# The per-chunk norm of a bidirectional scan: variance spread by its own product, root and reciprocal at full width

## The chip, the cores and the metric

The kernel runs on one core of a Trainium2 chip. The metric is the device time of one execution, in microseconds. TensorE (PE in the profile, its weight loads PEld), VectorE (DVE), ScalarE (ACT), GpSimd (POOL) and the DMA queues work in parallel and are kept in order by semaphores alone; on each engine instructions run in the order in which the program lists them.

## What is computed

One layer of a hybrid backbone over 1024 latent and 128 context tokens, 1024 channels, 16 heads of 64, all in fp32. The part that matters here is the norm at the end of the token mixer's scans:

```
wkv = ys[0] + ys[1]                     # forward and backward scan
mu = jnp.mean(wkv, axis=-1, keepdims=True)          # over a head's 64 channels
var = jnp.mean(jnp.square(wkv - mu), axis=-1, keepdims=True)
ln = ((wkv - mu) * lax.rsqrt(var + LNX_EPS)).reshape(B, T, D_RWKV) * p['lnx_w'] + p['lnx_b']
x_a = (ln + (bonuses[0] + bonuses[1]).reshape(B, T, D_RWKV)).astype(xn.dtype) * g_out
```

Around it stand the input projections ahead of the scans and, behind them, the output projections and the MLP.

## The kernel before

**Stages.** Projections of eight pairs of heads (to about 1035 us of the span), the scans (1035 to 1640 us), then dense products. Only the scans are touched, and of them only the norm.

**The scans.** A pair of heads is 128 channels, which lie on the 128 partitions, head 0 on the upper 64 and head 1 on the lower. Time is cut into NC = 9 chunks of C = 128 tokens, eight latent and one context. A unit is a pair and a chunk position; there are UNITS = 72, and both directions of a unit are done together. One software-pipelined loop, `for s in range(-4, UNITS)`, is written out for every engine: step s does the serial part of unit s, the Gram products of unit s + 4, and inverse work of the units between. With j = s mod 9, TensorE's order in a step is: turn (transposes into inv), token_major (transposes into bank 3), ur_state (the state's product, ser<-state,ub), gram of direction 0 (gbank<-ub), serial_ur (ser<-vb,gmat), **spread**, left (inv<-xtb), y_state (ser<-ub,state), gram of direction 1, serial_u, right, **mean**, serial_s, serial_y, **gate**, **variance**.

**The norm of a chunk.** `finals(s)` names the chunk whose y is complete in step s, one a step from s = 5 on (67 units); the last five are done in a tail behind the loop (`TAIL`). Per chunk, y is yf, 128 channels by 128 tokens:
- TensorE, mean: ones within a head (bones) times y, so that the sum stands on all 64 channels of the head (place(n, 0) in bank 2). VectorE, centred (L2180): y minus the mean. ScalarE, squares_of (L1675): the square into fsq, a ring of five buffers.
- TensorE, variance: fsq as the stationary operand and two columns of bones as the moving one. The result has the tokens on the partitions and the two heads as columns: 128x2, in two columns at the end of bank 2 (`column(n)`).
- ScalarE, deviation (L1681), at the start of the next step: the square root, 128x2, into fstd. VectorE, reciprocal (L2184): 128x2, in place.
- TensorE, spread, in the next step: each column of fstd, repeated 64 times, times the identity, which gives 1/deviation for every channel and token (place(n, 1) in bank 2). VectorE, scaled: y times that (L2189), weight and bonus (L2193), bias and gate (L2196), then the chunk goes out by DMA.

**What sets the order around it.** VectorE's order in step s: reciprocal of the last step's chunk, y_add (L2168, the sum of the two directions' y, for units with j = 4 to 7; the others are copied by ScalarE, L1666), turned (L2114), carried (L2142), the Gram mask of direction 0 (L2108), the three operations of scaled, summed (L2125), centred, states (L2157), the Gram mask of direction 1. In steps 9 to 23 a forward substitution for the last pair (L2029, L2036) is laced in, around scaled. TensorE's ur_state and first Gram product wait until the y of the unit before is out (yd_ok or ya_ok), its second Gram product for the mask of direction 0 (gram_ok), its y_state for ScalarE's copy of ur (ur_ok, L1651), its serial_u for GpSimd's triangle products (tri_ok, L898).

In the tail the five chunks go stage by stage: five means, five centrings, five squares, five gates, five variances, five roots, five reciprocals, five spreads, and then, behind all five spreads, five times scaled. The dense products need the last one's result.

The matmuls go through a helper and all bear L970; the tiles tell them apart.

## Time and profile before

| | before |
|---|---|
| median of 3 runs | 2705.92 us (2702.68 to 2709.07) |
| the profiled execution: time / span | 2705.67 us / 2703.6 us |
| busy in the span | PE 2580.1, PEld 2430.1, DVE 1852.0, ACT 1080.2, POOL 1175.8 us |
| granted TensorE clock, mean | 0.985 |
| the scans | 1035 to 1640 us of the span |

All durations come from the profiled execution, whose own time lies 0.25 us below the median. Matmuls are pipelined and up to four small ones run on different parts of the array at once, so a row's mean duration is not what it costs; the starts of the weight loads (PEld) show the pace. An fp32 product is two records, a product over both heads four.

### The profile page before, as it was taken

The page shows a single profiled execution, that of the slowest core. Times are in us where ns is not written, and L with a number is a line of the kernel's source. Part 1 is how long each engine was busy: PE and PEld are TensorE (multiplying, and loading weights), DVE is VectorE, ACT ScalarE, POOL GpSimd, SP SyncE. Part 2 cuts the span into 40 slices and gives each one's busy share as a digit, 9 for nine tenths or more (in the row PEclk, how much of TensorE's full clock was granted, in tenths as well). Part 3 has the DMA queues.
Part 4 walks back from the last instruction along what each step waited for, and adds up shares of the span by engine and source line. Part 5 has one row for each costly group of instructions (what it writes and reads, how often), then busy time and mean ns, then how long its engine had stood idle before and what let it go on. Part 6 is the DMA issues. An engine that isn't in the chain of part 4 may idle for free.

```text
span 2703.6 us, 68164 instructions
## 1 busy us (share of the span) xinstructions
PE 2580.1 (95%) x28864; PEld 2430.1 (90%) x28864; DVE 1852.0 (68%) x3010; ACT 1080.2 (40%) x1978; POOL 1175.8 (43%) x1154
## 2 busy tenths in 40 slices
PE   4899999999999998999999997999799999999998
PEld 3899999999999996788878887999799999999998
DVE  3464665846748464787766666799778679678686
ACT  3434243342433422433333343443453353443534
POOL 1323222322223224555555544656446556565662
PEclk8999999999999999999999999999899999999999
DMA  8333425435254363444454456454223232333231
GB/s 323 106 110 109 144 69 181 125 97 158 62 174 128 94 193 108 131 143 144 138 154 137 139 160 195 131 175 105 63 63 79 81 101 70 79 84 102 65 79 71
DMA packets 282412, 329.15 MB, mean 122 GB/s; under 512 B 76288, under 2 KB 215936, under 8 KB 273536
## 3 DMA queue, kind: packets, MB, share of 16 engines
q1 hardware_dynamic: 274448, 278.66, 33.2%
q0 software_dynamic: 5904, 39.32, 6.9%
q10 hardware_dynamic: 1760, 6.82, 0.6%
q8 instruction: 231, 3.78, 0.6%
q14 instruction: 69, 0.57, 0.1%
HBM read 221.83 MB, written 91.36 MB: 116 GB/s over the span
## 4 chain that ended last, share of the span: by engine, by line
PE 85%; DVE 7%; issue 2%; DMA 2%; ACT 2%; SPq 1%; POOL 0%; DVEq 0%; ACTq 0%; POOLq 0%
PE ser L970 18%; PE gbank L970 13%; PE bank L970 11%; PE inv L970 11%; PE gbank L1411 8%; PE inv L1411 8%; PE ser L1411 7%; PE bank L1411 7%; DVE a_sum L2298 1%; DMA ring<-in_wblocks 1%; PE inv L1172 1%; PE bank L1155 1%; DVE a_sum L2302 1%; DVE a_sum L2306 1%; DVE a_lo L2272 1%
## 5 line engine op out<-in xcount | busy, mean ns | idle before, releaser
L952 POOL TENSOR_TENSOR w_lo<-raw_w,w_hi 128x512 fp32r<-128x512 f32 x264 | 425.3, 1624 | 370.2 <-ACT w_hi L1747 370.1
L847 POOL TENSOR_TENSOR wsp<-ring,wsp 128x1024 fp32r<-128x1024 f32 x67 | 210.8, 3146 | 670.7 <-ACT wsp L1513 670.7
L1747 ACT ACTIVATE w_hi<-raw_w 128x512 fp32r<-128x512 f32 x264 | 165.1, 632 | 262.5 <-PE ser L1411 98.4
L970 PE MATMUL ser<-xn_hi,wsp 128*128 128x384 f32 x816 | 217.7, 340 | 6.1 <-POOL xn_lo L853 6.1
L1411 PE MATMUL gbank<-a_hi,w_hi 128*128 128x288 f32 x616 | 185.7, 302 | 30.6 <-POOL w_lo L952 14.6
L970 PE MATMUL gbank<-xn_hi,wsp 128*128 128x384 f32 x800 | 213.0, 339 | 1.1 <-issue 1.1
L970 PE MATMUL bank<-xn_hi,wsp 128*128 128x384 f32 x800 | 211.1, 338 | 2.2 <-POOL wsp L847 2.2
L970 PE MATMUL inv<-xn_hi,wsp 128*128 128x384 f32 x800 | 211.3, 338 | 0.5 <-issue 0.5
L2108 DVE TENSOR_TENSOR gmat<-gbank,gmask 128x1024 f32<-128x1024 f32 x144 | 175.6, 1219 | 49.8 <-PE gbank L970 49.0
L1733 ACT ACTIVATE a_hi<-a_sum 128x1152 fp32r<-128x1152 f32 x88 | 103.1, 1173 | 224.6 <-DVE a_sum L2306 78.0
L970 PE MATMUL gbank<-ub 64*64 64x128 f32 (+1 forms) x3456 | 178.4, 310 | 9.5 <-DVE gmat L2108 5.6
L1411 PE MATMUL gbank<-a_hi,w_lo 128*128 128x288 f32 x616 | 184.7, 300 | 0.0
L1411 PE MATMUL gbank<-a_lo,w_hi 128*128 128x288 f32 x616 | 184.4, 299 | 0.0
L1411 PE MATMUL inv<-a_hi,w_lo 128*128 128x288 f32 x616 | 183.9, 299 | 0.0
L1411 PE MATMUL inv<-a_hi,w_hi 128*128 128x288 f32 x616 | 183.7, 298 | 0.0
L1411 PE MATMUL inv<-a_lo,w_hi 128*128 128x288 f32 x616 | 183.6, 298 | 0.0
L1411 PE MATMUL ser<-a_hi,w_hi 128*128 128x288 f32 x616 | 181.6, 295 | 1.5 <-ACT r L1786 1.5
L1411 PE MATMUL bank<-a_hi,w_lo 128*128 128x288 f32 x616 | 181.8, 295 | 0.0
L1411 PE MATMUL ser<-a_hi,w_lo 128*128 128x288 f32 x616 | 181.7, 295 | 0.0
L1411 PE MATMUL ser<-a_lo,w_hi 128*128 128x288 f32 x616 | 181.4, 294 | 0.0
L1411 PE MATMUL bank<-a_lo,w_hi 128*128 128x288 f32 x616 | 181.4, 294 | 0.0
L1411 PE MATMUL bank<-a_hi,w_hi 128*128 128x288 f32 x616 | 181.3, 294 | 0.0
(398 smaller groups left out, 7534.7 us busy)
## 6 DMA issues: line engine op xcount, KB each, us to landing
ring<-in_wblocks SPq DMA_DIRECT2D x107, 512.0 KB, 4.8
ub<-op_d SPq DMA_DIRECT2D x144, 256.0 KB, 2.8
raw_w<-in_wquads SPq DMA_DIRECT2D x33, 1024.0 KB, 4.8
raw_w<-in_wquads POOLq DMA_DIRECT2D x22, 1024.0 KB, 8.8
op_d<-ar SPq DMA_DIRECT2D x32, 576.0 KB, 5.4
op_d<-bk SPq DMA_DIRECT2D x32, 576.0 KB, 6.2
raw_w<-in_wquads SPq DMA_DIRECT2D x44, 256.0 KB, 3.3
raw_w<-zsum POOLq DMA_DIRECT2D x11, 1024.0 KB, 12.3
```

What stands on the lines that cost most here:

```text
L847: GT(wsp[s % 2][1][:], ring[(N_ADA_RING + s) % RING][:], wsp[s % 2][0][:].bitcast(F32), ALU.subtract).then_inc(S["wsplit_lo"], 1)
L952: GT(w_lo[n % 4][:], src, w_hi[n % 4][:].bitcast(F32), ALU.subtract).then_inc(S["wl_ok"], 1)
L970: return nc.tensor.matmul(out, lhsT, rhs, start=start, stop=stop)
L1155: ins = nc.tensor.transpose(banks[3][:, y * P:(y + 1) * P], ub[v % LOADS][:, y // 2, 2 + y % 2, :], ident[:])
L1172: ins = nc.tensor.transpose(inv[:, 0, x * P:(x + 1) * P], xt[:, place_of(v), :, :].rearrange("p h t -> p (h t)"), ident[:])
L1411: return nc.tensor.matmul(out, lhsT, rhs, start=start, stop=stop, skip_group_check=True)
L1733: A(a_hi[:, places2(q, j), :], src, ACT.Copy).then_inc(S["ah_ok"], 1)
L1747: A(w_hi[s][:], raw_of(op)[:, m, :].rearrange("p (k c) -> p k c", k=KH), ACT.Copy).then_inc(S["wh_ok"], 1)
L2108: V.tensor_tensor(gmat[v % SETS][:, d, :, :, :].rearrange("p h x t -> p h (x t)"), gbank[:, :, :], gmask[:, d:d + 1, :].to_broadcast([P, 2 ...
L2272: V.tensor_tensor(a_lo[:, places2(q, j), :], src, a_hi[:, places2(q, j), :].bitcast(F32), sub).then_inc(S["al_ok"], 1)
L2298: ch.step(V.tensor_tensor(o[j], a11[j], a12[j], sub))
L2302: ch.step(V.tensor_tensor(o[j], o[j], a22[j], add))
```

## The change

- **variance** takes bones (the 64x64 block of ones of a head) as the stationary operand and fsq as the moving one: as in the mean, the sum stands on all 64 channels of the head, 128x128, in place(n, 1) of bank 2 (in the tail in banks 4 and 5).
- **deviation** reads that, takes the root of 128x128 and writes it over fsq, whose squares have been used. squares_of waits for the buffer's last user now, where deviation did.
- **reciprocal** works on 128x128 in fsq, in place.
- **spread** is gone, with its wait for the reciprocal, its ring fstd and its place in the tail; scaled multiplies by fsq from SBUF and waits for the reciprocal, which runs on its own engine.

The diff, without the declaration of fstd, the calls of spread and a semaphore count in a later norm that follows from it:

```
-            def column(n):
-
-                i = n - TAIL[0][2]
-                return banks[2][:, 4 * P - 2:4 * P] if i < 0 else ser[:, 1, 2 * i:2 * i + 2]
-
             def variance(p, c, n):
                 pe.wait_ge(S["ysq_ok"], n + 1)
-                for b in halves_of:
-                    ins = mm(column(n)[b, :], fsq[:, n % 5, b], bones[:, 0:P:HD], True, True)
+                for hs in halves_of:
+                    ins = mm(place(n, 1)[hs, :], bones[hs, hs], fsq[hs, n % 5, :], True, True)
                 ins.then_inc(S["var_full"], 1)
-
-            def spread(p, c, n):
-
-                pe.wait_ge(S["rec_ok"], n + 1)
-                for h in range(2):
-                    ins = mm(place(n, 1)[halves_of[h], :], fstd[:, n % 5, h:h + 1].to_broadcast([P, HD]), ident[:], True, True)
-                ins.then_inc(S["spread_full"], 1)
...
             def squares_of(p, c, n):
+                if n >= 5:
+                    act.wait_ge(S["xa_ok"], n - 4)
                 act.wait_ge(S["yc_ok"], n + 1)
                 A(fsq[:, n % 5, :], yf[p % 2][:, c * C:(c + 1) * C], ACT.Square).then_inc(S["ysq_ok"], 1)
 
             def deviation(p, c, n):
                 act.wait_ge(S["var_full"], n + 1)
-                if n >= 5:
-                    act.wait_ge(S["xa_ok"], n - 4)
-                A(fstd[:, n % 5, :], column(n), ACT.Sqrt, scale=1.0 / HD, bias=eps_t[:, 1:2]).then_inc(S["std_ok"], 1)
+                A(fsq[:, n % 5, :], place(n, 1), ACT.Sqrt, scale=1.0 / HD, bias=eps_t[:, 1:2]).then_inc(S["std_ok"], 1)
...
             def reciprocal(p, c, n):
                 dve.wait_ge(S["std_ok"], n + 1)
-                V.reciprocal(fstd[:, n % 5, :], fstd[:, n % 5, :]).then_inc(S["rec_ok"], 1)
+                V.reciprocal(fsq[:, n % 5, :], fsq[:, n % 5, :]).then_inc(S["rec_ok"], 1)
 
             def scaled(p, c, n):
                 y = yf[p % 2][:, c * C:(c + 1) * C]
-                dve.wait_ge(S["spread_full"], n + 1)
-                ch.step(V.tensor_tensor(y, y, place(n, 1), mul))
+                dve.wait_ge(S["rec_ok"], n + 1)
+                ch.step(V.tensor_tensor(y, y, fsq[:, n % 5, :], mul))
```

VectorE in step 6, from the second Gram mask of the step before to the scaling. Before:

```order
L2108 TENSOR_TENSOR gmat<-gbank,gmask 128x1024 [waits gram_full]
L2184 RECIPROCAL fstd<-fstd 128x2 [waits std_ok]
L2168 TENSOR_TENSOR yf<-ser,yf 128x2x128 [waits ya_ok,y_full]
L2114 TENSOR_TENSOR tc<-inv,trimc 128x384 [waits tr_full]
L2142 TENSOR_SCALAR stg<-state,gstep 128x64 [waits s_ok]
L2142 TENSOR_SCALAR stg<-state,gstep 128x64
L2108 TENSOR_TENSOR gmat<-gbank,gmask 128x1024 [waits gram_full]
L2189 TENSOR_TENSOR yf<-yf,bank 128x128 [waits spread_full]
```

Now:

```order
L2091 TENSOR_TENSOR gmat<-gbank,gmask 128x1024 [waits gram_full]
L2167 RECIPROCAL fsq<-fsq 128x128 [waits std_ok]
L2151 TENSOR_TENSOR yf<-ser,yf 128x2x128 [waits ya_ok,y_full]
L2097 TENSOR_TENSOR tc<-inv,trimc 128x384 [waits tr_full]
L2125 TENSOR_SCALAR stg<-state,gstep 128x64 [waits s_ok]
L2125 TENSOR_SCALAR stg<-state,gstep 128x64
L2091 TENSOR_TENSOR gmat<-gbank,gmask 128x1024 [waits gram_full]
L2172 TENSOR_TENSOR yf<-yf,fsq 128x128 [waits rec_ok]
```

The order is the same; the reciprocal is 128 columns wide, and the scaling waits for it and no longer for TensorE.

TensorE in the same step, from the end of the first Gram product to the second. Before:

```order
L970 MATMUL gbank<-ub 64x256 x4
L970 MATMUL ser<-vb,gmat 64x64 x8
L970 MATMUL bank<-ident,fstd 64x128 [waits rec_ok]
L970 MATMUL bank<-ident,fstd 64x128
L970 MATMUL inv<-xtb,gmat 64x64 [waits xtb_ok,tc_ok,lm3_ok,lm4_ok]
L970 MATMUL inv<-xtb,gmat 64x64 x3
L970 MATMUL inv<-xtb,lm 64x64 x8
L970 MATMUL ser<-ub,state 64x128 [waits ur_ok]
L970 MATMUL ser<-ub,state 64x128 x3
L970 MATMUL gbank<-ub 64x128 [waits gram_ok]
```

Now:

```order
L969 MATMUL gbank<-ub 64x256 x4
L969 MATMUL ser<-vb,gmat 64x64 x8
L969 MATMUL inv<-xtb,gmat 64x64 [waits xtb_ok,tc_ok,lm3_ok,lm4_ok]
L969 MATMUL inv<-xtb,gmat 64x64 x3
L969 MATMUL inv<-xtb,lm 64x64 x8
L969 MATMUL ser<-ub,state 64x128 [waits ur_ok]
L969 MATMUL ser<-ub,state 64x128 x3
L969 MATMUL gbank<-ub 64x128 [waits gram_ok]
```

The spread and its wait for the reciprocal are gone from between serial_ur and left; nothing else has moved.

## Rows read from the trace of the kernel before

**Rows 1.** Busy us of each engine in a stretch (instructions), granted clock, DMA share, GB/s:
```profile
core 0: us, PE busy (x) PEld busy (x) DVE busy (x) ACT busy (x) POOL busy (x), PEclk, DMA share, GB/s
1260.00:1560.00 300.00, 297.03 (x7406) 242.18 (x7408) 205.67 (x478) 114.74 (x315) 153.90 (x335) 1.00 0.47 141
```

**Rows 2.** Timeline of a step with a y sum: start us, us, engine, line, operation:
```profile
1463.56 0.25 PEld L970 LDWEIGHTS bank<-bones,fsq 128*64 128x64 f32 x4
...
1463.95 0.26 ACT L1681 ACTIVATE fstd<-bank,eps_t 128x2 f32<-128x2 f32 x1 [1.06 <-PE bank L970]
...
1464.32 0.15 DVE L2184 RECIPROCAL fstd<-fstd 128x2 f32<-128x2 f32 x1
1464.39 0.40 DVE L2168 TENSOR_TENSOR yf<-ser,yf 128x256 f32<-128x256 f32 x1
...
1464.85 0.32 PEld L970 LDWEIGHTS ser<-state,ub 64*64 64x64 f32 x16 [0.27 <-DVE yf L2168]
...
1466.11 0.55 PEld L970 LDWEIGHTS ser<-vb,gmat 128*64 128x64 f32 x16 [0.39 <-issue]
...
1466.25 1.22 DVE L2108 TENSOR_TENSOR gmat<-gbank,gmask 128x1024 f32<-128x1024 f32 x1 [0.56 <-PE gbank L970]
...
1466.57 0.20 PEld L970 LDWEIGHTS bank<-ident,fstd 128*64 128x64 f32 x4
...
1466.84 0.38 ACT L1651 ACTIVATE ur<-ser 128x256 f32<-128x256 f32 x1 [1.39 <-PE ser L970]
...
1466.95 0.21 PEld L970 LDWEIGHTS inv<-xtb,gmat 64*64 64x64 f32 x8 [0.17 <-issue]
...
1467.29 0.41 PEld L970 LDWEIGHTS ser<-ub,state 64*64 64x64 f32 x7
...
1467.57 0.14 PEld L970 LDWEIGHTS gbank<-ub 64*64 64x64 f32 x2
```

**Rows 3.** Who waited for the y sum (L2168): us in all, times:
```profile
  PEld ser L970: 8.0, 25
```

**Rows 4.** Timeline of TensorE's loads in step 1, which has no norm:
```profile
1050.44 0.55 PEld L970 LDWEIGHTS ser<-vb,gmat 128*64 128x64 f32 x16 [0.39 <-issue]
...
1051.61 0.41 PEld L970 LDWEIGHTS ser<-ub,state 64*64 64x64 f32 x7
...
1051.89 0.57 PEld L970 LDWEIGHTS gbank<-ub 64*64 64x64 f32 x15
```

**Rows 5.** Groups of instructions by line: busy us, mean ns of one | idle before:
```profile
L2057 DVE RECIPROCAL kk<-kk 128x1152 f32<-128x1152 f32 x8 | 58.8, 7353 | 0.3
L2184 DVE RECIPROCAL fstd<-fstd 128x2 f32<-128x2 f32 x72 | 11.4, 159 | 15.0 <-ACT fstd L1681 14.9
...
L1675 ACT ACTIVATE fsq<-yf 128x128 f32<-128x128 f32 x72 | 21.9, 309 | 5.7 <-DVE yf L2180 4.1
```

**Rows 6.** Timeline of VectorE in step 19, with the substitution:
```profile
1197.23 0.38 DVE L2036 TENSOR_TENSOR r<-r 72x110 f32<-72x110 f32 x1
1197.65 1.23 DVE L2108 TENSOR_TENSOR gmat<-gbank,gmask 128x1024 f32<-128x1024 f32 x1
```

**Rows 7.** Timeline of VectorE, first Gram mask in steps 2, 4 and 0 of later pairs:
```profile
1430.10 1.23 DVE L2108 TENSOR_TENSOR gmat<-gbank,gmask 128x1024 f32<-128x1024 f32 x1 [0.64 <-PE gbank L970]
...
1448.98 1.23 DVE L2108 TENSOR_TENSOR gmat<-gbank,gmask 128x1024 f32<-128x1024 f32 x1 [0.50 <-PE gbank L970]
...
1489.43 1.22 DVE L2108 TENSOR_TENSOR gmat<-gbank,gmask 128x1024 f32<-128x1024 f32 x1 [0.28 <-PE gbank L970]
```

**Rows 8.** Timeline of VectorE in the last step and in the tail:
```profile
1625.20 0.35 DVE L2193 SCALAR_TENSOR_TENSOR yf<-yf,pl,fbon 128x128 f32<-128x128 f32 x1 [0.74 <-DMA fbon<-bon_d]
...
1632.69 0.78 DVE L2184 RECIPROCAL fstd<-fstd 128x2 f32<-128x2 f32 x5 [1.03 <-ACT fstd L1681]
...
1634.33 0.29 DVE L2189 TENSOR_TENSOR yf<-yf,inv 128x128 f32<-128x128 f32 x1 [0.86 <-PE inv L970]
```

**Rows 9.** Lines L2193 and L898: count, duration ns min/median/max, first and last start:
```profile
L2193 DVE SCALAR_TENSOR_TENSOR yf<-yf,pl,fbon x72: 350/456/609, 1093.0 to 1638.5; 128x128 f32<-128x128 f32 x72
...
L898 POOL TENSOR_TENSOR tt<-xt,ttm x288: 416/424/478, 1034.3 to 1616.5; 64x128 f32<-64x128 f32 x144
```

More of the change, by code:

```diff
@@ L390, in flow_step @@
         mrow = sb(sc, "mrow", [P, MG])
-        fstd = sb(sc, "fstd", [P, 5, 2])
         fbon, fsq = (sb(sc, n, [P, 5, C]) for n in ("fbon", "fsq"))
@@ L1362, in _ @@
                         pe.wait_ge(S["ada_ok"], p + 1)
-                for x in finals(s - 1):
-                    spread(*x)
                 if inverses:
@@ L1388, in _ @@
                     variance(*x)
-            for x in finals(UNITS - 1):
-                spread(*x)
             pe.wait_ge(S["tok_ok"], UNITS)
@@ L1399, in _ @@
                 variance(*x)
-            for x in TAIL:
-                spread(*x)
             pe.wait_ge(S["xa_ok"], UNITS)
@@ L1666, in y_out, with place @@
                     A(y, ser[:, 1, 2 * P:(2 + n) * P].rearrange("p (n t) -> p n t", t=P), ACT.Copy).then_inc(S["ya_ok"], 1)
-            def column(n):
+            def place(n, k):
                 i = n - TAIL[0][2]
-                return banks[2][:, 4 * P - 2:4 * P] if i < 0 else ser[:, 1, 2 * i:2 * i + 2]
+                if i < 0:
+                    return banks[2][:, k * P:(k + 1) * P]
+                return banks[(0, 4, 2)[k] + i // 4][:, (i % 4) * P:(i % 4 + 1) * P]
             def squares_of(p, c, n):
+                if n >= 5:
+                    act.wait_ge(S["xa_ok"], n - 4)
                 act.wait_ge(S["yc_ok"], n + 1)
@@ L1784, in norm_copy @@
             def norm_copy(h):
-                act.wait_ge(S["spread_full"], UNITS + h + 1)
+                act.wait_ge(S["spread_full"], h + 1)
                 A(rs[h].rearrange("p (b t) -> p b t", b=2), ser[:, :, 0:GH], ACT.Copy).then_inc(S["rs_ok"], 1)
@@ L2242, in _ @@
             dve.wait_ge(S["gate_full"], UNITS)
-            dve.wait_ge(S["spread_full"], UNITS)
             for x in TAIL:
```

## The prediction

> **What bounds the kernel now.** The change touches only the scans, so I read the profile in this order: the busy times by stretch, the timeline of one step of the scans on all engines, the same for a step without the norm, and the list of who waits for whom. The scans run from 1035 to 1640 us. In their middle TensorE is busy 297.0 of 300 us, VectorE 205.7 [rows 1]. By that table anything taken from TensorE is a gain and VectorE has room. The timeline says otherwise. One step of the loop takes 7.5 to 8 us, and in it TensorE and VectorE hand work to each other four times; what counts is which hand-over comes last.
>
> In the step at 1464 us [rows 2] the order on VectorE is: the reciprocal of the norm (L2184), the y sum (L2168), the mask of the turned blocks, the carried state, the first Gram mask (L2108). The y sum ends at 1464.79 and TensorE starts its next product (ser<-state,ub) at 1464.85, after waiting for it. So in this kind of step the reciprocal lies on the path already: it stands ahead of the y sum in VectorE's queue. The profile counts 8.0 us in 25 times for this wait on the loads of ser alone [rows 3]. By the program it concerns the steps 5 to 8 of each pair's nine, 32 steps.
>
> In the other steps (0 to 4 of a pair) ScalarE moves y out and VectorE has no y sum; there VectorE waits for TensorE ahead of the first Gram mask, and that wait is its slack.
>
> **The removed product.** The spreading product starts at 1466.57, and the next product of TensorE (inv<-xtb) starts 0.38 us later, at 1466.95 [rows 2]. Taken as work, that is 0.38 us a step. But what follows it waits for others: the state's part of y starts at 1467.29, and ScalarE's copy of ur that it needs ended at 1467.22; the second Gram product starts at 1467.57, and VectorE's Gram mask that it needs ended at 1467.47. Both hang on products ahead of the spread, not on it. The trace has the proof in the first five steps, which have no norm and so no spread: there the same stretch from the 16 loads of ser<-vb,gmat to the state's part of y is 1051.61 - 1050.44 = 1.17 us, and 1.45 us to the Gram product [rows 4]; with the spread it is 1467.29 - 1466.11 = 1.18 and 1.46 [rows 2]. The spread is hidden to within 0.01 us. I cost its removal at nothing; what is late next is the copy of ur and the Gram mask, both at once.
>
> **The variance product.** Before: four loads over 0.25 us, two moving columns each. After: 64 rows on 64 columns, 128 moving; the nearest row is the spread with its 128 moving columns, four loads over 0.20 us [rows 2]. So between -0.05 and, if it came on top of the old one's time, +0.20 us a step, and nearest to the first, since the count of loads stays four; I take zero on the path, since VectorE's reciprocal mostly starts behind the Gram mask ahead of it and not at this product's end.
>
> **The root.** 128x2 takes 0.26 us; ScalarE's square of 128x128 takes 0.31 [rows 2, 5]. So 0 to 0.05 us more. It counts only where the reciprocal waits for ScalarE (step 4 and step 8 of a pair, some 14 steps), where it cancels against the product above.
>
> **The reciprocal.** This is the whole of the case. The trace has it at 2 columns (159 ns) and at 1152 (7353 ns) [rows 5]. The slope between them is 7194/1150 = 6.26 ns a column, so 128 columns take 0.159 + 126 x 6.26 ns = 0.95 us: 0.79 us more, in all 72 units. Bounds: in proportion to the long one, 7.353/9 = 0.82 (+0.66); proportion plus the short one's whole time, 0.98 (+0.82). An even lower end is that of any other 128x128 operation of VectorE, 0.29 us (+0.13) [rows 8]; two points on a line make that unlikely, and it is a rival below. I take +0.79.
>
> The Trainium skill (VectorE: DVE Perf Modes, "First, the fixed hardware budget" and "Specifications") describes the reciprocal as an iterated divide with a repeat count of 8, at 0.96 GHz; an estimate from that page is 8.3 ns a column, +1.05 us. The row at 1152 columns gives 6.26, so the trace goes below the page; by the page the sum would be about 17 us higher.
>
> **What it does, step by step.** A reciprocal is in steps 6 to 71 of the 72, 66 in all, and in the five units of the tail.
> - Steps 5 to 8 of a pair, 31 of them with a reciprocal: the y sum ends 0.79 us later, TensorE stands for it, and VectorE's later work moves along with TensorE, so nothing is won back. 31 x 0.79 = 24.5 us. Behind TensorE's wait stand the Gram products, the serial products and the next step's turn.
> - Steps 0 to 4 of pairs 1 and 2 (10 steps) carry the forward substitution as well. There VectorE reaches the Gram mask with almost no wait: its last small operation ends at 1197.61, the mask starts at 1197.65 [rows 6]. Operations of VectorE follow each other some 0.08 us before the one ahead is reported done (the y sum starts at 1464.39, the reciprocal ends at 1464.47), so the slack is 0.12 us. A late mask holds the second Gram product: 10 x (0.79 - 0.12) = 6.7 us.
> - Steps 0 to 4 of pairs 3 to 7: the wait ahead of the mask is 0.28 us in step 0, 0.64 in steps 1 to 3, 0.50 in step 4 [rows 7]; with the 0.08, slack of 0.36, 0.72 and 0.58. Left over: 5 x 0.43 + 15 x 0.07 + 5 x 0.21 = 2.2 + 1.0 + 1.1 = 4.3 us.
> - The tail: five roots, five reciprocals, then five scalings. Now the first reciprocal starts at 1632.69 and the scalings at 1634.33, with the spreading products between them [rows 8]. After: reciprocals 0.87 apart from 1632.73, the last done at 1632.73 + 4 x 0.87 + 0.95 = 1637.16, the scalings at about 1637.1, without a spread between. +2.8 us, and the dense products wait for the last scaling.
> - Given back: in the last step VectorE waits 0.74 us for the bonus from memory [rows 8], and that landing doesn't move: -0.7.
>
> Sum: 24.5 + 6.7 + 4.3 + 2.8 - 0.7 = **+37.6 us**. On the profiled execution's 2705.67 (span 2703.6) that is 2743.3; the median of the runs, 2705.92, is 0.25 away, so **2743 us**, +1.4%.
>
> With only the bounds of the reciprocal's cost (+0.66 to +0.82) the same sum runs from +29 to +40, that is 2735 to 2745.
>
> **Rivals.**
> - *Every added nanosecond arrives*: the slack ahead of the Gram masks isn't one, since something else ends there too (the carried state's own waits, say). 66 x 0.79 + 2.8 = +55: 2761. For it: four hand-overs per step are within 0.1 us of each other. Against: the waits in [rows 7] are for TensorE alone. Chance 0.07.
> - *The spread's time does come back*: TensorE gains 0.38 in each step though two waits end there. Then the terms become 31 x 0.41 + 10 x 0.29 + 5 x 0.05 - 15 x 0.31 - 5 x 0.17 + 2.8 = +13: 2719. Against it stand [rows 2, 4]. Chance 0.04.
> - *GpSimd is held up*: the scaling now reads two operands from SBUF, where one came from PSUM, beside GpSimd's triangle products (L898), whose end the next serial product awaits closely. The other operation with two such operands (L2193) varies from 350 to 609 ns, so there is contention; but it is VectorE that gives way, L898 stays within 416 to 478 [rows 9]. If instead GpSimd lost the scaling's 0.28 us in each of the 35 steps where TensorE doesn't wait for a y sum: +9.8, 2753. Chance 0.06. The rule behind it is in the Trainium skill (SBUF — State Buffer, "Who interferes with whom"): a VectorE instruction with two SBUF inputs contends with a GpSimd instruction that reads SBUF. By that rule the trace agrees for VectorE's side only.
> - *The reciprocal is cheap at 128 columns*: +0.13 us as for other operations. Then 31 x 0.13 = +4.0, the slacks cover the rest, and the tail gains some 0.5: 2709, no change that can be told. Chance 0.03.
> - *Faster, the other side*: the same cheap reciprocal and the spread's time won too. The mechanism is a TensorE that is full, as [rows 1] has it, so that four fewer matmuls a unit shorten every step: -67 x 0.38 + 4.0 - 0.5 = -22: 2684. It decides as soon as the reciprocal adds less than 0.38 us and the copy of ur isn't the last to arrive. Chance 0.02.
>
> **The numbers.** The forecast has 0.78. Rivals that are slower have 0.17 together, no change 0.03, faster 0.02. A measurement of this kernel can tell about 0.2% (5.4 us) from no change. Slower by more than that: 0.78 + 0.17 = 0.95, of which I keep 0.01 for mishaps that I haven't thought of: 0.94, same 0.03, faster 0.03. The range takes in the bounds of the reciprocal, some error in the slacks (all of them gone for 20 steps is +11), and the GpSimd rival; it ends short of the two outer rivals: 2730 to 2758, which holds about 0.84.
>
> **What would show it.** The reciprocal's row should read 0.9 to 1.0 us for 128x128. TensorE's waits for the y sum (L2168 in the list of who waits) should grow from 8.0 us in the row for ser to some 27 there. The stretch from ser<-vb,gmat to the second Gram product should stay at 1.46 us without the spread. VectorE's wait for gbank ahead of the first Gram mask should be near zero in steps 1 to 3 of a pair. TensorE's busy share in the scans should fall by some 5 points. If steps 5 to 8 of a pair aren't about 0.8 us longer each, the forecast is wrong at its main term; if steps 1 to 3 get shorter, the spread wasn't hidden.

## The result and the profile after

| | before | after |
|---|---|---|
| median of 4 runs, us | 2706.19 (2702.68 to 2709.07) | 2761.40 (2758.12 to 2763.05) |
| ratio (95% interval) | 1 | 1.0203 (1.0185 to 1.0221) |
| span of the profiled execution, us | 2703.6 | 2760.1 |

The change makes the kernel 55 us slower. The forecast was 2743 with a range up to 2758; the time lies 18 us above the one and 3 above the other. "Slower" was right, and so was the reciprocal's price. What was wrong is the rest of the step.

The middle of the scans by stretch, to be read against [rows 1] (columns as there):

```profile
1260.00:1560.00 300.00, 284.11 (x6723) 221.24 (x6719) 215.93 (x440) 109.50 (x290) 141.80 (x310) 1.00 0.45 130
```

TensorE is busy 284 of 300 us where it was 297, so 4.3 points fewer (the forecast said some 5), and fewer steps fit in the stretch. The groups of instructions by line, and then who waited for whom, with us in all, times and the longest (against [rows 5] and [rows 3]):

```profile
L2167 DVE RECIPROCAL fsq<-fsq 128x128 f32<-128x128 f32 x72 | 68.1, 950 | 35.3 <-ACT fsq L1664 35.3
...
L1664 ACT ACTIVATE fsq<-bank,eps_t 128x128 f32<-128x128 f32 x67 | 24.6, 368 | 97.0 <-PE bank L969 97.0
```

```profile
DVE fsq L2167 <- ACT fsq L1664: 35.3, 61, 2.4
...
PEld ser L969 <- DVE yf L2151: 27.1, 25, 2.0
```

The reciprocal takes 950 ns; 0.95 us was forecast. TensorE's wait for the y sum went from 8.0 to 27.1 us in the same 25 times; some 27 was forecast. But the root takes 368 ns, not about 310, and VectorE now stands 35.3 us in 61 places for it, where it stood 14.9 us in 20 for the short one. That is new. VectorE's wait ahead of the first Gram mask in steps 1 to 3 of the later pairs, 0.64 us in [rows 7], is gone, as forecast. The timeline of the step that [rows 2] shows, in the changed kernel (start us, us, engine, line, operation):

```profile
1500.64 1.22 DVE L2091 TENSOR_TENSOR gmat<-gbank,gmask 128x1024 f32<-128x1024 f32 x1
...
1500.80 0.25 PEld L969 LDWEIGHTS bank<-gl,pl 128*64 128x64 f32 x4
...
1501.22 0.20 PEld L969 LDWEIGHTS bank<-fsq,bones 64*64 64x64 f32 x4 [0.17 <-issue]
...
1501.59 0.31 PEld L1171 LDWEIGHTS inv<-ident,xt 128*128 128x128 f32 x3 [0.17 <-issue]
...
1501.70 0.37 ACT L1664 ACTIVATE fsq<-bank,eps_t 128x128 f32<-128x128 f32 x1 [1.39 <-PE bank L969]
...
1502.10 0.95 DVE L2167 RECIPROCAL fsq<-fsq 128x128 f32<-128x128 f32 x1 [0.25 <-ACT fsq L1664]
...
1502.97 0.36 DVE L2151 TENSOR_TENSOR yf<-ser,yf 128x256 f32<-128x256 f32 x1
...
1503.39 0.32 PEld L969 LDWEIGHTS ser<-state,ub 64*64 64x64 f32 x16 [1.06 <-DVE yf L2151]
...
1504.65 0.55 PEld L969 LDWEIGHTS ser<-vb,gmat 128*64 128x64 f32 x16 [0.39 <-issue]
...
1505.27 0.21 PEld L969 LDWEIGHTS inv<-xtb,gmat 64*64 64x64 f32 x8
...
1505.82 0.41 PEld L969 LDWEIGHTS ser<-ub,state 64*64 64x64 f32 x7
...
1506.10 0.13 PEld L969 LDWEIGHTS gbank<-ub 64*64 64x64 f32 x1
```

and the three rows of the kernel before that belong beside its first, second and fourth (the second Gram mask, the gate's loads and the turn's; the variance product's row and the root's stand in [rows 2]):

```profile
1463.19 1.22 DVE L2108 TENSOR_TENSOR gmat<-gbank,gmask 128x1024 f32<-128x1024 f32 x1
...
1463.35 0.25 PEld L970 LDWEIGHTS bank<-gl,pl 128*64 128x64 f32 x4
...
1463.83 0.31 PEld L1172 LDWEIGHTS inv<-ident,xt 128*128 128x128 f32 x3
```

Two things are to be seen. The lower end of the step is as forecast: from the 16 loads to the state's part of y 1.17 us, to the Gram product 1.45, as in [rows 4] and without the spread. The upper end isn't. From the gate's loads to the turn's went 0.48 us and now go 0.79; the variance product, which has tiles of 64 rows and 64 columns (64\*64) between a gate of 128\*64 and a turn of 128\*128, has a pause of 0.17 us ahead of it and one behind it. From the gate's loads to the root's start went 0.60 us and now go 0.90. The forecast had set both at zero.

To compare kernels I measured each step from its second Gram mask to the next one's, in the timeline of VectorE, and took the difference from the kernel before. Medians of the three kinds of step, in us, and the sum over steps 6 to 67 (the sums carry single pauses of 1 to 2 us that come at other steps in each profile; the medians don't):

| kernel | ratio to before | y sum (5 to 8) | substitution (0 to 4, pairs 1, 2) | steps 1 to 3, later pairs | sum of 62 steps |
|---|---|---|---|---|---|
| the change | 1.0203 | 1.07 | 1.27 | 0.34 | 50.8 |
| e1, variance product 128\*64 | 1.0167 | 0.92 | 0.79 | 0.13 | 36.8 |
| e7, that and root of 2 columns | 1.0148 | 0.81 | 0.81 | 0.12 | 34.3 |
| e8, variance product 128\*128 | 1.0218 | 1.11 | 1.27 | 0.34 | 54.9 |
| e12, GpSimd's copies narrowed | 1.0181 | 1.07 | 0.61 | 0.27 | 42.4 |
| e2, reciprocal of 2 columns | 1.0081 | 0.34 | 0.27 | 0.27 | 19.1 |
| e10, e1 with reciprocal past the y sum | 1.0074 | 0.21 | 0.79 | 0.13 | 17.0 |
| e5, reciprocal past the Gram mask | 1.0061 | 0.17 | 0.27 | 0.27 | 14.6 |
| e6, e1 with reciprocal past the Gram mask | 1.0024 | 0.03 | 0.12 | 0.12 | 4.2 |
| e9, e5 with variance product moved | 1.0030 | 0.02 | 0.11 | 0.11 | 5.9 |
| e4, before with variance product 64\*64 | 1.0021 | 0.11 | 0.14 | 0.14 | 9.3 |
| e3, before without the spread | 0.9980 | -0.03 | -0.03 | -0.03 | -2.7 |
| e11, before, reciprocal past the y sum | 0.9991 | -0.06 | 0.00 | 0.00 | -0.9 |

### The profile page after: what moved, and what is told of

Its sections match the earlier page's. It is cut to its first block, busy times and chain, and to the rows that moved or that the text cites. A ratio compares the mean times of both kernels' runs of the same rounds, so it can differ in the third digit from the quotient of the medians.

```text
span 2760.1 us, 67582 instructions
## 1 busy us (share of the span) xinstructions
PE 2599.9 (94%) x28576; PEld 2425.3 (88%) x28576; DVE 1908.8 (69%) x3010; ACT 1087.9 (39%) x1978; POOL 1178.9 (43%) x1154
## 4 chain that ended last, share of the span: by engine, by line
PE 83%; DVE 9%; issue 3%; ACT 2%; DMA 2%; SPq 1%; POOL 0%; DVEq 0%; ACTq 0%; POOLq 0%
PE ser L969 18%; PE gbank L969 13%; PE bank L969 11%; PE inv L969 11%; PE gbank L1392 8%; PE inv L1392 7%; PE ser L1392 7%; PE bank L1392 7%; DVE a_sum L2280 1%; DMA ring<-in_wblocks 1%; DVE a_sum L2284 1%; DVE a_sum L2288 1%; DVE gmat L2091 1%; DVE a_lo L2254 1%; ACT fsq L1664 1%
```

## The experiments

My theory from this trace: the reciprocal costs what was forecast, and the excess comes from the variance product's tile shape and the longer root. The rival is the forecast's own, that every added nanosecond of reciprocal arrives: it had named 2761.

### Which product shape, on the change: e1

```diff
-    ins = mm(place(n, 1)[hs, :], bones[hs, hs], fsq[hs, n % 5, :], True, True)
+    ins = mm(place(n, 1)[hs, :], bones[:, hs], fsq[:, n % 5, :], True, True)
```

> The changed kernel with its variance product as two tiles of 128 rows and 64 columns (all of the block matrix's rows, of which the other head's are zero; same result), the shape of the gate products ahead of it, where the change has 64 rows and 64 columns. Theory A (the shape costs: in the trace of the changed kernel the gate begins at 1500.80, the variance product at 1501.22 and the turn of y at 1501.59, 0.79 us in all, with two gaps of 0.17 us put down to issue, against 0.48 us in the kernel before): gate to turn is 0.48 to 0.55 us again, the root starts some 0.25 us earlier against the second Gram mask, and some 64 steps get 0.25 to 0.31 us back, 16 to 20 us: 2741 to 2746 us. Theory B (all of the excess over the forecast is reciprocal time that no slack absorbs; the products' shape is off the path): 2758 to 2763 us as the changed kernel.

Ratio 1.0167 (1.0143 to 1.0191), span 2744.8: 15 us less than the change in the profiled executions, 10 by the ratios. The timeline:

```profile
1488.97 0.25 PEld L969 LDWEIGHTS bank<-gl,pl 128*64 128x64 f32 x4
...
1489.19 0.25 PEld L969 LDWEIGHTS bank<-fsq,bones 128*64 128x64 f32 x4
...
1489.61 0.31 PEld L1171 LDWEIGHTS inv<-ident,xt 128*128 128x128 f32 x3 [0.17 <-issue]
...
1489.73 0.37 ACT L1664 ACTIVATE fsq<-bank,eps_t 128x128 f32<-128x128 f32 x1 [1.24 <-PE bank L969]
...
1490.13 0.95 DVE L2167 RECIPROCAL fsq<-fsq 128x128 f32<-128x128 f32 x1
...
1491.42 0.31 PEld L969 LDWEIGHTS ser<-state,ub 64*64 64x64 f32 x14 [1.06 <-DVE yf L2151]
```

With the gate's shape one of the two pauses is gone: 0.64 us from gate to turn, not the 0.48 to 0.55 that I expected, and the root starts after 0.76 us where it was 0.90. The steps with a y sum get 0.15 us shorter, as much as the root is earlier. So the shape is a cause, with 0.15 us a step and not 0.25 to 0.31. The intervals of this run and of the change just meet (1.0191 and 1.0185), so it is the steps that speak against the rival, by which nothing would move.

### The other shape: e8

```diff
-    for hs in halves_of:
-        ins = mm(place(n, 1)[hs, :], bones[hs, hs], fsq[hs, n % 5, :], True, True)
-    ins.then_inc(S["var_full"], 1)
+    mm(place(n, 1), bones[:], fsq[:, n % 5, :], True, True).then_inc(S["var_full"], 1)
```

> The changed kernel with its variance product as one tile of 128 rows by 128 columns with the whole block matrix (same result), the shape of the turn of y behind it. Theory A (the two gaps of 0.17 us come from a change of tile shape, so one gap at the border gate to variance is left, or none where 128 rows meet 128 rows): gate to turn 0.45 to 0.65 us, and 9 to 14 us less than the changed kernel, as with the tile of 128 rows by 64 columns: ratio to the kernel before 1.015 to 1.018. Theory B (64 columns is what matters, or the gaps come with the wait for the squares): 0.79 us from gate to turn, and 1.020.

Ratio 1.0218 (1.0201 to 1.0234). Gate to turn is what I expected and the time isn't:

```profile
1481.18 0.25 PEld L969 LDWEIGHTS bank<-gl,pl 128*64 128x64 f32 x4
...
1481.60 0.30 PEld L969 LDWEIGHTS bank<-fsq,bones 128*128 128x128 f32 x2 [0.17 <-issue]
...
1481.82 0.36 PEld L1171 LDWEIGHTS inv<-ident,xt 128*128 128x128 f32 x3
...
1482.13 0.37 ACT L1662 ACTIVATE fsq<-bank,eps_t 128x128 f32<-128x128 f32 x1 [1.41 <-PE bank L969]
```

There is one pause here too, but ahead of the product and not behind it, and it is 0.64 us to the turn as in e1. Yet the root starts 0.95 us after the gate's loads, against 0.76 in e1 and 0.90 in the change. The steps with a y sum follow the root's start and not the turn's: 1.11, 0.92 and 1.07 us. This corrected my reading of e1: in these steps a pause counts if it stands ahead of the norm's chain (product, root, reciprocal, y sum); the one behind the product is hidden by TensorE's own wait for the y sum. The table has the same hint for steps 1 to 3 of the later pairs: e8 costs 0.34 us there and e1 0.13, though the turn is as early in both.

### The same shape on the kernel before: e4

```diff
-    ins = mm(column(n)[b, :], fsq[:, n % 5, b], bones[:, 0:P:HD], True, True)
+    ins = mm(column(n)[b, :], fsq[b, n % 5, b], bones[b, b.start:b.start + 2], True, True)
```

> The kernel before with its variance product over 64 rows in place of 128 (half of each sum is left out, so the norm is wrong by it), 2 columns wide as before; reciprocal, root and spreading product stay. Only the tile's shape is that of the changed kernel. Theory A (a product of another tile shape between the gate and the turn costs two gaps of 0.17 us on TensorE, whatever it computes): gate to turn goes from 0.48 to 0.75 to 0.8 us, and the time rises by 0.2 to 0.31 us in some 60 steps, 12 to 19 us: 2718 to 2725 us. Theory B (the 128 columns cost, not the shape, or nothing does): 2704 to 2709 us.

Ratio 1.0021 (1.0010 to 1.0032), so 5.7 us, against 12 to 19 expected. The step gets 0.11 us longer where there is a y sum and 0.14 elsewhere. The loads say why it is half of what I expected: the pause stands ahead of the product, and none behind it.

```profile
1475.72 0.25 PEld L970 LDWEIGHTS bank<-gl,pl 128*64 128x64 f32 x4
...
1476.15 0.20 PEld L970 LDWEIGHTS bank<-bones,fsq 64*64 64x64 f32 x4 [0.17 <-issue]
...
1476.36 0.31 PEld L1172 LDWEIGHTS inv<-ident,xt 128*128 128x128 f32 x3
```

Nothing but the tiles' shape differs (and with it that half of each sum is left out), with two moving columns as before, and it costs a good 0.1 us in every kind of step. So a border between tile shapes costs by itself. The second pause of the change is not seen here, behind two moving columns; in the change 128 stand ahead of it.

### The reciprocal and the root by themselves: e2, e7

```diff
-    V.reciprocal(fsq[:, n % 5, :], fsq[:, n % 5, :]).then_inc(S["rec_ok"], 1)
+    V.reciprocal(fsq[:, n % 5, 0:2], fsq[:, n % 5, 0:2]).then_inc(S["rec_ok"], 1)
```

> The changed kernel with the reciprocal taken of 2 of its 128 columns (the other 126 keep the root: the norm's reciprocal is left out there), so the variance product in 64-row tiles and the root over 128 columns stay. Theory A (the product's shape and the longer root cost by themselves, about 0.31 and 0.11 us a step, of which the steps in which y's sum is waited for pay): the reciprocal gives back 0.79 us in about 37 steps and part of it elsewhere, 33 to 39 us, and 2722 to 2728 us are left, 16 to 22 us above the kernel before. Theory B (the reciprocal is all of it): 2704 to 2710 us, as the kernel before.

Ratio 1.0081 (1.0063 to 1.0099), profiled at 2725.9. In a step with a y sum 0.73 us comes back, in steps 1 to 3 of later pairs 0.07. What stays is 0.34 and 0.27 us a step: product and root, without any reciprocal to speak of. This is the run that the rival can't pass: it wanted the time of the kernel before.

```diff
-    ins = mm(place(n, 1)[hs, :], bones[hs, hs], fsq[hs, n % 5, :], True, True)
+    ins = mm(place(n, 1)[hs, :], bones[:, hs], fsq[:, n % 5, :], True, True)
...
-    A(fsq[:, n % 5, :], place(n, 1), ACT.Sqrt, scale=1.0 / HD, bias=eps_t[:, 1:2]).then_inc(S["std_ok"], 1)
+    A(fsq[:, n % 5, 0:2], place(n, 1)[:, 0:2], ACT.Sqrt, scale=1.0 / HD, bias=eps_t[:, 1:2]).then_inc(S["std_ok"], 1)
```

> The changed kernel with the variance product of 128 rows by 64 columns, and the root taken of 2 columns in place of 128 (the reciprocal then takes 126 columns of squares: root and norm are left out there). Theory A (the root's 0.11 us sits ahead of the reciprocal in every step): 0.09 to 0.11 us less than with the 128-row product alone in some 60 steps, 5 to 7 us: a ratio to the kernel before of 1.013 to 1.015 where the 128-row product alone gave 1.0167. Theory B (the root is covered by VectorE's mask): no difference from that one.

Ratio 1.0148 (1.0132 to 1.0165). The interval meets that of e1, so the steps have to speak: with a y sum 0.81 us where e1 has 0.92, which is the root's 0.11; in the other steps nothing (0.81 for 0.79, 0.12 for 0.13). There the root is covered. With the short root and one of the two pauses gone, the steps with a y sum cost 0.81 us: the forecast had 0.79.

### The removed product: e3

```diff
-    for x in finals(s - 1):
-        spread(*x)
...
-    dve.wait_ge(S["spread_full"], n + 1)
-    ch.step(V.tensor_tensor(y, y, place(n, 1), mul))
+    dve.wait_ge(S["rec_ok"], n + 1)
+    ch.step(V.tensor_tensor(y, y, fsq[:, n % 5, :], mul))
```

> The kernel before without its spreading product: the norm's multiplication by the spread reciprocal is made with the squared channels instead (so the norm is left out of the result), and everything else stays. Theory A (TensorE's spreading work of 0.2 us a step, and its wait for the reciprocal, lie where TensorE waits for VectorE's masks anyway): 2704 to 2708 us, no change. Theory B (it holds TensorE up at the step's start, so its removal should have given 0.2 to 0.4 us a step back, and the changed kernel's cost is larger than it seems by that much): 2681 to 2694 us.

Ratio 0.9980 (0.9968 to 0.9991), 0.03 us a step of the 0.38 that the product seems to take, in every kind of step. The spread was hidden, as the forecast read from [rows 2, 4]; what its removal can give is about 2 us in the steps and at most 9 by the interval.

### GpSimd beside VectorE: e12

In the substitution steps the change costs 1.27 us, more than the reciprocal, and e1 gives 0.48 of it back, more than the root's earlier start. VectorE's rows in such a step, first in the kernel before (the rows that follow stand in [rows 6]), then in the change:

```profile
1196.39 0.62 DVE L2142 TENSOR_SCALAR stg<-state,gstep 128x64 f32<-128x64 f32 x2
1196.93 0.26 DVE L2029 TENSOR_TENSOR r<-r 72x110 f32<-72x110 f32 x1
```

```profile
1210.25 0.85 DVE L2125 TENSOR_SCALAR stg<-state,gstep 128x64 f32<-128x64 f32 x2
1211.03 0.54 DVE L2012 TENSOR_TENSOR r<-r 72x110 f32<-72x110 f32 x1
1211.61 0.47 DVE L2019 TENSOR_TENSOR r<-r 72x110 f32<-72x110 f32 x1
1211.99 1.21 DVE L2091 TENSOR_TENSOR gmat<-gbank,gmask 128x1024 f32<-128x1024 f32 x1
```

and GpSimd's beside them:

```profile
1210.63 1.73 POOL L897 TENSOR_TENSOR tt<-xt,ttm 64x128 f32<-64x128 f32 x4
```

The two small operations take 0.54 and 0.47 us for 0.26 and 0.38, and the carried state (stg, two operations) 0.85 for 0.62. The whole stretch of VectorE is later by the reciprocal, and so it meets GpSimd's four copies. In e1, where the stretch starts 0.15 us earlier, the carried state reads 0.62 us again (median of the ten steps), which is half of what e1 gives back there. The edit makes these short:

```diff
-    GT(tt[v % 2][b, d, :, b], xt[b, place_of(v), :, :], two(ttm[b, d, :]), ALU.mult)
+    GT(tt[v % 2][b, d, :, b.start:b.start + 4], xt[b, place_of(v), :, 0:4], two(ttm[b, d, :])[:, :, 0:4], ALU.mult)
```

> The changed kernel with GpSimd's four masked copies of a step (tt<-xt, 0.43 us each, 1.70 us in all) made of 4 of their 64 columns: the triangles' other columns are left out, so what the products make of them isn't the reference's; everything else stays. In the changed kernel VectorE's carried state runs beside them and takes 0.85 us for its two instructions where it took 0.62, and the substitution's two small operations 0.54 and 0.47 us for 0.26 and 0.38. Theory A (VectorE is slowed by GpSimd's operations that it now meets): the carried state falls to 0.5 to 0.7 us, the substitution's operations to 0.26 to 0.38, and the substitution steps from 1.27 us over the kernel before to 0.9 to 1.0; the y steps, in which VectorE waits for the first Gram mask anyway, don't change; in all 4 to 6 us less, ratio 1.018 to 1.019. Theory B (their length comes from elsewhere): the durations stay, ratio 1.020.

```profile
1209.64 0.63 DVE L2125 TENSOR_SCALAR stg<-state,gstep 128x64 f32<-128x64 f32 x2
1210.19 0.31 DVE L2012 TENSOR_TENSOR r<-r 72x110 f32<-72x110 f32 x1
1210.53 0.27 DVE L2019 TENSOR_TENSOR r<-r 72x110 f32<-72x110 f32 x1
1210.72 1.21 DVE L2091 TENSOR_TENSOR gmat<-gbank,gmask 128x1024 f32<-128x1024 f32 x1
```

The substitution steps fall from 1.27 to 0.61 us, more than I expected, and the steps with a y sum keep their 1.07. The whole is 1.0181 (1.0160 to 1.0202), whose interval includes the change's 1.0203; by the steps it is 8.4 us. VectorE's own rows carry the verdict: 0.85, 0.54 and 0.47 us became 0.63, 0.31 and 0.27 without any edit on VectorE, 0.65 us together, about as much as the step got shorter. The Trainium skill (SBUF — State Buffer, "Who interferes with whom") says that VectorE operations with two SBUF inputs contend with GpSimd's that read SBUF, and that those in its two-port modes contend with GpSimd's too; the trace agrees, by these durations. The forecast cited that section and asked only whether GpSimd would be held up. It was VectorE again, and on the path.

### Where the reciprocal stands: e5, e10, e6

e5 moves the reciprocal from the step's start to just ahead of the scaling:

```diff
     for s in range(-4, UNITS):
-        for x in finals(s - 1):
-            reciprocal(*x)
         if there(s) and j == 4:
+            for x in finals(s - 1):
+                dve.wait_ge(S["std_ok"], x[2] + 1)
...
         if there(s + 4):
             gram(s + 4, 0)
         for x in finals(s - 1):
+            reciprocal(*x)
             scaled(*x)
```

> The changed kernel with the reciprocal moved on VectorE from the step's start to just ahead of the multiplication that uses it, behind the first Gram mask; all is computed, and where the step has the add of the modulations it waits for the root as before. Theory A (the reciprocal's 0.95 us cost time only because the y sum and the turn of the products stand behind it, as does VectorE's 0.25 us of waiting for the root): behind the mask it falls into the 1.0 to 1.1 us in which VectorE waits there for TensorE's block products. The variance product's 0.31 us on TensorE is left and meets the 0.27 us by which TensorE waited for the y sum in the kernel before: 0 to 0.15 us a step, and 3 to 5 us at the end of the scans: 2706 to 2720 us. Theory B (VectorE is full there, so 0.8 us more of work costs 0.8 us wherever it stands): 2755 to 2763 us, as the changed kernel.

Ratio 1.0061 (1.0046 to 1.0077), span 2720.7: 39 us less than the change for an edit that takes no work away. That is the answer to "VectorE is full". What is left is TensorE's: 0.27 us in the steps without a y sum. It is the product's 0.31 longer way to the turn less the spread's 0.03, whole. There TensorE has no slack, while in the steps with a y sum most of it is under the old wait for the y sum (0.17 left).

e10 takes e1 and moves the reciprocal only past the y sum:

```diff
         if there(s - 1):
             y_add(s - 1)
+        for x in finals(s - 1):
+            reciprocal(*x)
```

> The changed kernel with the variance product of 128 rows by 64 columns (ratio 1.0167 to the kernel before) and the reciprocal moved only past the y sum, so that the turned products' mask, the carried state and the first Gram mask stay behind it; all is computed. Theory A (each place has its own slack: the y sum has none, the first Gram mask has 0.56 us in the steps with a y sum and about 0 to 0.5 in the substitution steps): the 31 steps with a y sum go from 0.92 us over the kernel before to 0.3 to 0.5 us, the other steps keep theirs (0.85 and 0.12): 13 to 19 us less, ratio 1.010 to 1.012. Theory B (VectorE is full): ratio 1.0167 as without the move. Theory C (only the y sum counts): as with the reciprocal behind the Gram mask in the y steps, ratio 1.006.

Ratio 1.0074 (1.0059 to 1.0090). The steps with a y sum fall from 0.92 to 0.21 us, more than the 0.3 to 0.5 that I expected, the others keep 0.79 and 0.13 to the hundredth. Each position has its own slack: ahead of the y sum none, ahead of the first Gram mask in those steps about 0.7 us of the 0.8, in the substitution steps next to none. (I had not counted that the mask's product comes 0.15 us later too.)

e6 is e5 with e1's product besides:

```diff
-    ins = mm(place(n, 1)[hs, :], bones[hs, hs], fsq[hs, n % 5, :], True, True)
+    ins = mm(place(n, 1)[hs, :], bones[:, hs], fsq[:, n % 5, :], True, True)
```

> As the run before (reciprocal behind the first Gram mask), and the variance product as two tiles of 128 rows and 64 columns besides; all is computed. Theory A: both causes that the first runs point to are gone, TensorE has no spreading product and VectorE's y sum waits for nothing of the norm: 2700 to 2710 us, the kernel before or a little under it. Theory B (VectorE full): 2741 to 2752 us.

Ratio 1.0024 (1.0014 to 1.0033), 11 runs. VectorE's rows in a step with a y sum:

```profile
1479.65 0.41 DVE L2151 TENSOR_TENSOR yf<-ser,yf 128x256 f32<-128x256 f32 x1
1480.25 0.56 DVE L2097 TENSOR_TENSOR tc<-inv,trimc 128x384 f32<-128x384 f32 x1 [0.18 <-PE inv L1171]
1481.75 1.23 DVE L2091 TENSOR_TENSOR gmat<-gbank,gmask 128x1024 f32<-128x1024 f32 x1 [0.94 <-PE gbank L969]
1482.89 0.94 DVE L2167 RECIPROCAL fsq<-fsq 128x128 f32<-128x128 f32 x1
1483.87 0.29 DVE L2172 TENSOR_TENSOR yf<-yf,fsq 128x128 f32<-128x128 f32 x1
```

VectorE waits 0.94 us for TensorE again ahead of the mask, and the reciprocal, as long as ever, is behind it. The steps stand 0.03 and 0.12 us over the kernel before. 0.12 is about the 0.16 us that gate to turn is longer here (0.64 for 0.48) less 0.03. The time was to be 2700 to 2710 and is 2715, 6 us over the kernel before. In the profiled executions, whose spans differ by 8.7 us, 4.2 are in the 62 steps and 6.7 behind them; the steps ahead of them took 2.2 less.

### Could it be made level: e9, e11

e9 puts the 64\*64 product beside others of its own shape:

```diff
         if there(s + 1):
             token_major(s + 1)
+        for x in finals(s - 1):
+            variance(*x)
         if serial:
             ur_state(s)
...
         for x in finals(s):
             gate(*x)
-            variance(*x)
```

and on ScalarE

```diff
-        for x in finals(s - 1):
-            deviation(*x)
         if there(s - 1):
             y_out(s - 1)
         if there(s + 1):
             tokens(s + 1)
+        for x in finals(s - 1):
+            deviation(*x)
```

> All is computed; the reciprocal stands behind the first Gram mask as in the two runs before, and the variance product, with the change's tiles of 64 rows and 64 columns, is moved on TensorE from between the gate and the turn of the products to behind the token products of the next step, ahead of the state products that have the same 64-row tiles; ScalarE takes its root behind the copy of the tokens. Theory A (what the product costs TensorE is the border between tile shapes, so that beside products of its own shape it costs its columns alone): the 0.27 us a step that the late reciprocal with this product between gate and turn left in the steps without a y sum goes to 0 or below, the time to 0 to 5 us above the kernel before (the end of the scans), 2704 to 2713 us where before is 2706 to 2709. Theory B (four products with 128 columns cost that wherever they stand, or the later root holds the reciprocal up): 2714 to 2725 us.

Ratio 1.0030 (1.0019 to 1.0042), 8 us: more than theory A's 0 to 5, just within theory B's range, and no better than e6.

```profile
1478.09 0.25 PEld L969 LDWEIGHTS bank<-gl,pl 128*64 128x64 f32 x4
...
1478.51 0.31 PEld L1171 LDWEIGHTS inv<-ident,xt 128*128 128x128 f32 x3 [0.17 <-issue]
...
1479.43 0.14 PEld L969 LDWEIGHTS bank<-fsq,bones 64*64 64x64 f32 x2 [0.17 <-issue]
1479.45 0.14 PEld L969 LDWEIGHTS gbank<-ub 64*64 64x64 f32 x2
```

The pause between gate and turn stays, since these two have different shapes themselves; in the kernel before, the two-column product between them had none behind it. The step keeps 0.11 us. From the transposes ahead of the moved product (bank<-ident,ub) to ser<-vb,gmat it is 2.10 us where e5, without the product there, has 1.90: so four products with 128 columns cost 0.20 us beside their own shape, and 0.20 less 0.06 of gate to turn and 0.03 of the spread is the 0.11. I had counted the columns at nothing. The later root costs as well: in the steps 4 of later pairs, where VectorE waits for it ahead of another operation, e9 is 0.54 us over the kernel before and e5 0.27.

e11 makes e10's move on the kernel before:

```diff
-        for x in finals(s - 1):
-            reciprocal(*x)
         if there(s) and j == 4:
+            for x in finals(s - 1):
+                dve.wait_ge(S["std_ok"], x[2] + 1)
...
         if there(s - 1):
             y_add(s - 1)
+        for x in finals(s - 1):
+            reciprocal(*x)
```

> The kernel before with its reciprocal of 2 columns behind the y sum in place of ahead of it; all is computed, and the spreading product stays. Theory A (the y sum is what TensorE waits for; the reciprocal holds it up 0.07 us in the trace, and the spreading product has room): up to 0.07 us in 31 steps, 0 to 2 us less: 2704 to 2709 us, which can't be told from no change. Theory B (the wait for the root is part of it): 3 to 8 us less. If the spreading product's later start holds TensorE up: 2 to 6 us more.

Ratio 0.9991 (0.9980 to 1.0001), 12 runs against 21; 0.06 us less in each step with a y sum, as the 0.07 of [rows 2] allow. A gain of 0.1% is under what can be told here. No version that I ran beats the kernel before by more.

## Why the prediction was wrong

**The mechanism stood.** Reciprocal 0.95 us: measured 0.950. Spread hidden: e3 and the unchanged 1.17 and 1.45 us. The reciprocal ahead of the y sum on the path, and slack ahead of the Gram masks elsewhere: e10 and e5. With the short root and one pause less (e7) the 62 steps cost 34.3 us, and the forecast's terms for them are 27 x 0.79 + 6.7 + 4.3 = 32.3. Part of that closeness is luck: by kinds of step e7 has 22.1 us for 21.3 with a y sum, 9.9 for 6.7 in the substitution steps and 2.2 for 4.3 in steps 0 to 4 of the later pairs.

**The step that failed is "The variance product", with "The root".** The forecast bounded the product by -0.05 to +0.20 us, took its lower end by the count and length of its four loads, and put it at zero on the path. It cost 0.31 us of TensorE's time and delayed the root by 0.30. It looked at the rows of the product and not at the pauses between rows of unlike shape; [rows 2] has such a pause, 0.17 us ahead of inv<-xtb (64\*64) behind the 128\*64 spread, marked as issue. The root was priced by ScalarE's square (309 ns) and measured 368: +0.11 for +0.05 at most. The forecast then said that both count only where VectorE waits for ScalarE, in some 14 steps; the wait is there in 61 places now. It read that from the old chain, in which the reciprocal started 0.11 us behind the root's end, and did not add the new delays to it. 0.30 and 0.11 us, less some 0.08 of room, is 0.33 us by which the reciprocal starts later behind the Gram mask's start (1.13 us in the kernel before, 1.46 now, by the two timelines). With the reciprocal's 0.79 and a y sum that is 0.05 shorter that makes the 1.07 us of the step. The same sum gives 0.93 us for e1 (root 0.16 later and 0.11 longer), 1.12 for e8 (0.35 and 0.11) and 0.82 for e7 (0.16 and nothing); measured are 0.92, 1.11 and 0.81.

By kinds of step, over the forecast, from the medians: 27 x (1.07 - 0.79) = 7.6 us with a y sum; 10 x (1.27 - 0.67) = 6.0 in the substitution steps, where VectorE also meets GpSimd (e12 takes off 0.66 a step); 7.2 - 4.3 = 2.9 in steps 0 to 4 of later pairs, where TensorE's 0.27 us arrive whole (e5) and the forecast looked at VectorE's slack alone. That is 16.5 of the 50.8 - 32.3 = 18.5 us; the rest are single pauses.

**The end of the scans.** From the second Gram mask of step 67 to the first of the last five reciprocals went 29.5 us and now go 36.0: +6.5, where the forecast has four steps with a y sum and the bonus, 4 x 0.79 - 0.7 = +2.5. Of the 4.0 us between, 1.1 are the four steps' 0.28 each, and 1.2 are TensorE's clock, below: from the first token product to the gate 2.6 us for 1.4. Another 1.1 lie behind the loop, where the reciprocal of the last step's chunk stands: from it to the five it takes 5.2 us where it took 4.1. The forecast counted 66 reciprocals and five, and there are 72; this one was left out. What is left is about the 0.7 us that it took off for the bonus: that wait is gone, but nothing shows the time won. These shares are read from the rows, not separated by a run. From the first of the five to the first dense product went 11.8 us and now go 14.5: +2.7, forecast +2.8. The steps ahead of step 6 took 2.6 us less and the dense products 0.9 less, a scatter that other profiles have too (the first from 4.9 less to 4.1 more). In all, over the forecast: 18.5 + 4.0 - 0.1 - 2.6 - 0.9 = 18.9, and the profiled executions differ by 56.5 - 37.6 = 18.9.

**The rivals.** "Every added nanosecond arrives" named the time, 2761, and is wrong: it wanted e2 at the kernel before and e5 at the change. That it hit the number is a coincidence of 18 us of other costs. "GpSimd is held up" had the right pair of engines and the wrong one waiting. The range was built around the reciprocal's bounds, the one price that was firm, and left out the forecast's own +0.20 for the product: 0.20 us in 66 steps is +13, which takes the forecast alone to 2756.

## To carry to other kernels

Price an added product with the borders it makes to its neighbours: look at the tile shapes in the rows on both sides, and at the first operation that waits for its end, not at its own duration. When an operation in a chain gets longer, add up the delays of the whole chain up to the engine that next waits, even where each link looks covered. And ask of a long operation where in its engine's order it stands: the same 0.95 us cost 33 to 39 us more at the step's start than behind the mask (e1 and e6, the change and e5, by their spans).

## What the runs showed of the hardware

**A border between tile shapes.** A pause of 0.17 us on the loads stands ahead of a product whose tile shape differs from the one before (128\*64 to 64\*64, 128\*64 to 128\*128, 64\*64 to 128\*128, 128\*128 to 64\*64 in the rows above), where that one has 128 moving columns; behind a two-column product there is none in the rows (before, e4). In these rows the pause goes with the moving columns of the product ahead: behind the Gram product of direction 0, which ends with four products of 256 columns, it is 0.39 us ([rows 2, 4], ahead of ser<-vb,gmat), and behind ser<-vb,gmat with its 64 columns the loads of inv<-xtb,gmat follow after 0.07 us in the change (1504.65 + 0.55 to 1505.27), where behind the spread's 128 columns it was 0.17. The Trainium skill (TensorEngine Tiling (Array Packing), "Key Properties") says that changing the tiling mode drains the engine; the trace agrees so far as there is a pause at these borders, and this was the rule that spoke against the change and that the forecast didn't weigh.

**The root's price.** 262 ns at 2 columns and 368 at 128 make 0.84 ns a column. The square of the same 128 columns takes 309. The Trainium skill (ScalarE: Activation LUTs, "What ACT_TABLE_LOAD costs") gives 0.833 ns a column and some 93 ns more for an activation whose bias is an operand in memory, as the root's is; the rows differ by 59 ns, so the trace agrees in kind and not in size. The two also read from different memories, the root from PSUM and the square from SBUF, which no run here separates.

**TensorE's clock at the end.** Three stretches of the change (columns as in [rows 1]):

```profile
1670.00:1677.00 7.00, 4.53 (x90) 3.30 (x84) 2.59 (x7) 2.53 (x8) 0.00 (x0) 1.00 0.47 151
1677.00:1682.00 5.00, 4.95 (x68) 4.30 (x70) 0.77 (x3) 0.87 (x3) 0.00 (x0) 0.66 0.49 148
1682.00:1687.00 5.00, 3.42 (x56) 2.79 (x52) 2.94 (x9) 1.49 (x8) 0.00 (x0) 1.00 0.27 76
```

Ahead of the middle one TensorE was busy 4.5 of 7 us and stood 1.7 us for the y sum; then the granted clock is 0.66 in the mean, part of it at the lower level of 1.2 GHz, and eight products of ser<-gmat,up take 1.07 us:

```profile
1679.12 1.07 PE L969 MATMUL ser<-gmat,up 128*64 128x128 f32 x8
```

They take 0.61 us in the same place of the kernel before and of e6, whose clock stays at 1.00 there. It is tempting to say that TensorE's longer waits brought the lower clock, but the other profiles don't bear that out. e12 and e8 have the same waits there (1.7 us for the y sum, then 0.57) and keep 1.00; the drop is in the profiles of e2 and e5 too, and in that of e11, which is no slower than the kernel before and stood 0.24 us for the y sum. e12, then e11:

```profile
1673.18 0.61 PE L969 MATMUL ser<-gmat,up 128*64 128x128 f32 x8
...
1621.28 1.07 PE L970 MATMUL ser<-gmat,up 128*64 128x128 f32 x8
```

So the cause of the drop is open, and its 1.2 us belong to the profiled execution of the change rather than to the change.
